# Third group of token tiles multiplied as one unit of 384 columns, the products of ones between the tiles removed, 72 put ahead of the first, and a new order of the whole program

## What is computed

```python
u = rmsnorm(x, norm_g)
proj = u @ w_in                       # 1024 -> 8704 columns
lx, lg, sb, scg, sh, sg, q, qg, mg = jnp.split(proj, SPLIT_POINTS, axis=-1)
# A: causal conv(4) -> gated linear recurrence, SiLU gate
xc = causal_dwconv(lx, lru_buf, lru_conv_w) + lru_conv_b
hs = rglru(xc, lru_h, ...);  z_a = (hs * silu(lg)) @ lru_wo
# B: B * conv3(C * h), SiLU gate
z_b = (silu(sg) * sb * causal_dwconv(scg * sh, sc_buf, sconv_w)) @ sconv_wo
# C: cross-attention of 4 heads into 256 memory tokens, SiLU gate
z_c = (softmax(q @ mem_k.T / sqrt(128)) @ mem_v * silu(qg)) @ xa_wo
y = (g_a * z_a + g_b * z_b + g_c * z_c) @ w_out;  out = rmsnorm(x + y, final_norm_g)
```

## Time and profile before

| what | value |
|---|---|
| median of 3 runs | 723.51 us (722.99 to 723.92) |
| the profiled execution, its own time | 723.84 us |
| its span on the slowest core, 5 | 722.2 us (the cores: 719.7 to 722.2) |
| TensorE busy | 700.2 us, 97% of the span |
| VectorE, ScalarE, GpSimd busy | 402.2, 336.9, 172.8 us |
| chain of work that ended last | 93% TensorE |

### The profile page before, as it was taken

How to read it: one execution, slowest core, us unless ns; L and a number is a source line. 1 busy time by engine, 2 the same in 40 slices (tenths; PEclk the granted TensorE clock), 3 DMA queues, 4 the chain that set the end, 5 groups by cost and what they waited for, 6 DMA issues and landing times.

```text
span 722.2 us, 13551 instructions; the slowest of 8 cores (719.7 to 722.2 us)
## 1 busy us (share of the span) xinstructions
PE 700.2 (97%) x5097; PEld 462.7 (64%) x5097; DVE 402.2 (56%) x416; ACT 336.9 (47%) x435; POOL 172.8 (24%) x210
## 2 busy tenths in 40 slices
PE   4899999999999999999999999999999999999996
PEld 3887766666666666666666666666666666665443
DVE  3545206566958869886866879732213312134667
ACT  2664426888986795885931121231221121210535
POOL 3432200000000000000000635644516270732000
PEclk9999999999999999999999999999999999999998
DMA  8972493133133322343043677662356392277736
GB/s 190 259 217 31 106 157 90 30 63 56 17 54 59 58 40 52 57 70 49 10 107 55 121 177 178 143 100 37 46 77 105 49 136 45 30 170 235 239 140 241
DMA packets 32416, 73.99 MB, mean 102 GB/s; under 512 B 4464, under 2 KB 8880, under 8 KB 32096
## 3 DMA queue, kind: packets, MB, share of 16 engines
q0 software_dynamic: 18000, 31.60, 30.3%
q1 hardware_dynamic: 14352, 41.52, 17.7%
HBM read 90.73 MB, written 9.88 MB: 139 GB/s over the span
## 4 chain that ended last, share of the span: by engine, by line
PE 93%; DMA 3%; ACT 1%; DVE 1%; issue 1%; SPq 0%; POOL 0%; ACTq 0%; DVEq 0%; POOLq 0%
PE PP L739 75%; PE PP L1348 8%; PE PP L783 6%; PE PP L834 1%; DMA R<-xp 1%; DMA R<-memp 1%; PE PP L1092 1%; PE PP L1026 1%; PE PP L1113 1%; DMA R<-w_in 1%; DVE R L842 1%; ACT R L822 0%; PE PP L1227 0%; PE PP L1100 0%; ACT R L1078 0%
## 5 line engine op out<-in xcount | busy, mean ns | idle before, releaser
L739 PE MATMUL PP<-R 128*128 128x344 bf16 x3768 | 557.3, 309 | 1.6 <-ACT R L947 0.5
L739 PEld LDWEIGHTS PP<-R 128*128 128x128 bf16 x3768 | 366.9, 98 | 187.5 <-issue 6.9
L1285 ACT ACTIVATE R<-PP 128x688 f32<-128x688 f32 x72 | 53.4, 745 | 219.9 <-PE PP L739 197.4
L1294 DVE SCALAR_TENSOR_TENSOR R<-R,PP 128x688 f32<-128x688 f32 x72 | 62.5, 869 | 133.8 <-PE PP L739 130.1
L141 POOL DMA_DIRECT2D R<-w_in x68 | 39.1, 575 | 294.8 <-PE PP L739 196.4
L783 PE MATMUL PP<-R 128*128 128x128 bf16 (+3 forms) x672 | 56.6, 242 | 4.0 <-issue 2.0
L1348 PE MATMUL PP<-R 128*128 128x512 bf16 x256 | 55.4, 379 | 0.0
L783 PEld LDWEIGHTS PP<-R 128*128 128x128 bf16 x672 | 46.6, 100 | 11.1 <-issue 5.2
L1298 POOL TENSOR_TENSOR R<-R 128x688 f32<-128x688 f32 x24 | 40.5, 1687 | 20.8 <-DVE R L1294 20.4
L1303 POOL TENSOR_TENSOR R<-R 128x688 bf16<-128x688 f32 x24 | 42.3, 1772 | 12.8 <-DVE R L1294 11.2
L1348 PEld LDWEIGHTS PP<-R 128*128 128x128 bf16 x256 | 25.0, 98 | 30.1
(11 more groups left out here) (139 smaller groups left out, 517.7 us busy)
## 6 DMA issues: line engine op xcount, KB each, us to landing
R<-w_in POOLq DMA_DIRECT2D x68, 256.0 KB, 4.5
R<-xp SPq DMA_DIRECT2D x32, 512.0 KB, 9.1
R<-ck SPq DMA_DIRECT2D x16, 512.0 KB, 4.8
y_p<-R SPq DMA_DIRECT2D x16, 512.0 KB, 3.3
R<-R SPq DMA_DIRECT2D x64, 64.0 KB, 2.0
R<-cv POOLq DMA_DIRECT2D x16, 256.0 KB, 7.5
R<-w_out POOLq DMA_DIRECT2D x8, 256.0 KB, 7.4
R<-xa_wo POOLq DMA_DIRECT2D x14, 128.0 KB, 3.0
```

The source lines that it names most:

```text
L739: return lambda e: e.matmul(ps.ap[:, b * 512:b * 512 + BLK], lhs(k), rhs[:, k, c:c + BLK], start=(k == 0), stop=(k == nk - 1))
L1285: G.act(lambda e, ps=pg[u], th_=th_: e.activation(out=b3(th_.ap), in_=pv(ps), func=AF.Tanh, scale=0.5), UW, [pg[u].tok], [th_.tok], Px - E ...
L1294: G.dve(lambda e, zp=zp, th_=th_, dst=dst: e.scalar_tensor_tensor(out=b3(dst.ap), in0=b3(th_.ap), scalar=1.0, in1=pv(zp), op0=ALU.add, op1 ...
```

## The change

- `BYTILE` is 2: the third group (tiles 6, 7 and 8, columns 768 to 1152) of the seven finely cut projections is 8 products of 384 columns instead of 24 of 128.
- `FILL` is empty: no product of ones between or behind the tiles.
- `WARM` = 72 products of ones run ahead of the transposes of tile 0.
- The planner gets a table of arrivals (`ARRIVE`), by which in its model the first loads of a queue land no sooner, another cost for VectorE's product L1185 (1190 instead of 1024), and a new table `SHIFT`. These emit nothing; they set the order.

```diff
-WARM = 96
-FILL = (5, 5, 3, 2)
+WARM = 72
+ARRIVE = {
+    "sp": (5.0, 5.2, 9.5, 13.8, 16.8, 20.2, 23.1, 26.6, 29.8, 33.2, 36.2, 39.3, 42.4, 45.8, 48.8),
+    "pool": (9.1, 13.1, 16.4, 19.5, 22.8, 26.2, 29.4, 33.4, 36.9, 40.1, 43.4, 47.0),
+}
+FILL = ()
-BYTILE = 3
+BYTILE = 2
 SHIFT = {
-    "x0.act": 8, "x0.pool": -123, "x0.dve": 89.5, "x0.pe": -77, "x1.act": 138.5, "x1.pool": 52.5, "x1.dve": -97, "x1.pe": -87.5,
+    "first0.pool": -16.5, "x0.act": -1, "x0.pool": -16, "x0.dve": -1, "x1.act": -30, "x1.pool": -52, "x1.dve": 44.5, "x1.pe": -35.5,
...
+        landed = {q: list(v) for q, v in ARRIVE.items()}
...
+                if start < 58.0 and landed[q]:
+                    fin = max(fin, landed[q].pop(0))
...
-        G.pe([lambda e: e.matmul(warm.ap[:, 0:128], onesb, onesb, start=True, stop=True) for _ in range(1)], 7.0, [m_ones.t], [warm.tok], -300)
+        G.pe([lambda e: e.matmul(warm.ap[:, 0:128], onesb, onesb, start=True, stop=True) for _ in range(WARM)], 0.1, [m_ones.t], [warm.tok], -300)
...
-                    in1=qs.unsqueeze(1).to_broadcast([128, 8, 128]), op=ALU.mult), 1024, [k_.tok, m_qs.t], [pr_.tok], P1)
+                    in1=qs.unsqueeze(1).to_broadcast([128, 8, 128]), op=ALU.mult), 1190, [k_.tok, m_qs.t], [pr_.tok], P1)
```

More of the change, by code:

```diff
@@ L221 @@
 SHIFT = {
[12 rows of a table removed]
-    "kv.pool": 8.5, "kv.pe": 13, "kv.act": -10.5, "kv.sp": 29, "kv.dve": 89.5, "gates0.pe": 14, "gates0.act": 48, "rec0.act": -20.5,
[59 rows of a table removed]
[9 rows of a table added]
+    "x18.dve": 6, "x18.pe": 18.5, "states.sp": -13, "states.dve": -1, "states.act": 52, "states.pool": 19.5, "heads_q0.act": -4.5,
+    "heads_q1.pe": 16.5, "heads_q1.act": -2, "heads_q2.pe": 25.5, "heads_q2.act": -83.5, "heads_q3.pe": 22.5, "qs.dve": -1, "qs.pe": 50.5,
+    "A_lg0.pe": 58, "A_lg0.act": 158.5, "B_sg0.pe": -3, "A_lx0.dve": -8, "A_lx0.pe": -35.5, "A_lx0.act": -100, "conv0.act": -70.5,
+    "conv0.dve": -135.5, "kv.pool": 27, "kv.pe": 0.5, "kv.act": 2.5, "kv.sp": 9, "kv.dve": 2, "gates0.pe": -2.5, "gates0.act": -10.5,
[58 rows of a table added]
 }
@@ L838, in p0 @@
                 fill = Handle(PS, 1)
-                t = G.pe([lambda e, fill=fill: e.matmul(fill.ap[:, 0:128], onesb, onesb, start=True, stop=True) for _ in range(1)], 0.224,
+                t = G.pe([lambda e, fill=fill: e.matmul(fill.ap[:, 0:128], onesb, onesb, start=True, stop=True) for _ in range(4)], 0.224,
                          [m_ones.t], [fill.tok], 900)
```

## The result

The changed kernel takes 724.73 us, the median of 20 runs, beside 723.63 us for the kernel before, also 20 runs: the ratio is 1.0016, with a 95% interval of 1.0009 to 1.0024. So it is slower by about 1.2 us, less than the 0.2% that I had called no change, but on the other side of zero from the forecast of 1.0 us gained. (Two of the 20 executions, of 765 and 766 us, were disturbed on one half of the chip and are in no ratio.)

The account below looks back on a forecast made before the run. TensorE was taken as the bound, busy 700.2 of 722.2 us. Gains of 0.27 + 0.17 + 0.6 = 1.0 us off the median of 723.51 gave 722.5 us, range 720.0 to 725.5.

Parts of the forecast that it names:

- The rest of the order: Whole program: waits redrawn by the new order (`SHIFT`), taken as 0; bounds 1.5 us gained, 4 lost.
- First and second term: Where TensorE is full: fewer products through 384 columns, 0.27 us gained; three late products of ones dropped, 0.17 us.
- The front: Start up to tile 7: dropping the ones between tiles changes nothing; bounds 0.5 us gained, 1.0 lost.
- The instruction blocks: TensorE's early gaps awaiting instructions: 1.4 us against 2.03, 0.6 gained; bounds 2.0 gained, 1.0 lost.
- Rival 1: Faster: instruction gaps go on all cores, and some small waits too; 720.6 or 720 us, chance 0.32.
- Rival 2: At merge00: last recurrence comes late, a stall of 3 us gives 725.5; chance 0.16, including other waits this size.
- Rival 3: At the front: TensorE's clock falls again without ones between tiles, 1.6 us late at tile 7; 724.7 us, chance 0.12.

Follow-up runs that it names:

- before_again: The kernel before, run again with no edit; 723.45 us, ratio 0.9997.
- held_one: held_early with one product of ones at the start instead of 72; 721.71 us, ratio to the kernel before 0.9970.
- held_early: Changed kernel with six xp loads held until the fourth fix product is done and merge10's w_in load issued one GpSimd sum earlier; 721.56 us, ratio 0.9971.
- held_ones: held_early with 68 products of ones put back between the first tiles, where TensorE was idle; 722.09 us, ratio to the kernel before 0.9982.
- w_early: Changed kernel with only merge10's w_in load issued ahead of one GpSimd sum, 4.3 us earlier; 725.22 us, ratio to the kernel before 1.0014.

## Why the prediction was wrong

**The time**: 722.5 forecast, 724.73 measured, inside the range of 720.0 to 725.5, and near the price of the slower rivals.

**The step that failed** is "The rest of the order: I take 0". It has two parts, and both are real. The small waits of the old order are gone, which is what its lower bound promised: 0.17, 0.17, 0.41 and 0.49 us of core 3 are down to nothing. But the new order brought waits for loads, 2.0 to 4.2 us in sum on one core of each pair, and the time is that of the slowest core. I had put the bounds at 1.5 gained and 4 lost, which held, and had bounded the loss by a VectorE scan. I looked for the late result on VectorE and ScalarE and didn't look at how much earlier than its first product each weight load is issued on GpSimd, nor at what SyncE issues beside it. Both can be read from the new order: three GpSimd sums directly ahead of merge10's load and six ck loads around it, six xp loads directly beside the fix loads. What no row of the old kernel shows is how much longer a load takes in such company; the runs show 6.3 to 6.7 us instead of 2.7 to 3.0 for 128 KB on the later cores.

**The choice of 0 from what the old order showed** was the error in reasoning. That an order by the same planner had 1.6 us of waits says nothing about the next one: the planner models one core, and has no term for what its neighbour loads.

**First and second term**: 384 columns cost 162.5 ns in the changed kernel too (16 products from 41.32 to 43.92 us on core 3), no ones lie in the full stretch. Right, as far as the trace can show.

**The front**: forecast 0 with 1.0 lost as the bound; 0.76 us later on core 3. Of the idle time reckoned from tile 1 on, core 3 has 0.62 and 0.92 us behind the transposes of tiles 1 and 2, where I took 1.0 each; the 0.8 and 1.1 us ahead of tiles 2 and 3 didn't come, since TensorE with its slow products was itself the later one.

**The instruction blocks**: the forecast named the place, 123 products behind the first, behind tile 6's transposes, and none at 24 us. Right on both. The size was 0.71 us where I took 1.4 against 2.03 before. By the longest gaps of the two profiled executions the term gained 1.3 instead of 0.6, but the 2.03 was one execution's: before_again has 1.21 at most. Nor are these gaps the whole difference between the old kernel's cores, as I had it: core 5 is 2.5 us longer than core 3 and its gap 2.03, core 1 is 0.4 longer with a gap of 0.63. That the ones at the start are what removes the first gap I can't maintain: held_one has 1 product of ones and no gap there, so the new order does it, or chance.

**Rival 1** happened on the short cores: 718.5 to 719.2 us, below the best core before. It is what the kernel would be without the load waits, as held_early shows.

**Rival 2**, the last recurrence late to merge00, didn't happen: no wait there on any core. The time to spare was enough; how much of the 3.3 us was left isn't measured. The price of 725.5 was nearly right by luck, for another mechanism made the kernel slower.

**Rival 3**, the clock falls again, happened, and cost half of what I gave it, 0.76 instead of 1.6 us at tile 7: on core 3 some six eights went at the slow pitch, and not sixteen, for the products are fast again from about 19 us on. The Trainium skill (TensorE: Matmul & The Clock Gate, Part 1) has TensorE fall back to half rate when it is idle; here the rows at 13.46 and 15.95 agree. With held_ones, where the clock stays up, the spans don't fall, so this rival was right in its mechanism and not what made the kernel slower.

**Core 3 by these terms**: -0.27 - 0.17 + 0.76 - 1.24 + 0.11 (the last wait of the tail, 2.96 instead of 2.85) = -0.8 us; measured 719.7 to 719.2, -0.5. The 0.3 us between them aren't explained.

## What to carry to other kernels

When an order is made anew, list for every load the time from its issue to its first use and what else is issued beside it on any queue, and compare the shortest ones with the old order: a 128 KB load with 4.7 us of lead was in time alone on every core, and 1.6 to 2.0 us late on four of eight beside six loads of 512 KB. Bulk loads for a later stage are best tied to the end of the last small load's use, not left to whenever their buffers come free. Look at all cores of a profile, not at the slowest: a difference between neighbours that the program doesn't make points to something they share.

## What was unexpected of the hardware

- Of two neighbouring cores one was later in all 72 pairs of the changed kernel, by 3.0 us in the median, where both run the same program on their own data. It is not always the same one. With the two colliding loads untangled the difference is 0.5 us. That they share a path to memory is the reading that fits; no run measured that path itself. The Trainium skill (HBM Reference, Specifications) says that the two cores of a pair share the bandwidth of their memory, and advises to measure a change in transfers with both cores active. That the spans differ by pairs agrees with it; what either core of a pair got of the memory wasn't measured.
- A wait of TensorE in the middle of the kernel can cost more than itself. Behind 2.00, 2.34 and 2.80 us of idleness 32 products of 344 columns took 6.47 to 6.50 instead of 4.83 us (w_early), at a granted clock of 0.67 and 0.77 in the windows behind the last of these, and behind 5.60 us the clock was at 0.50. The length of the wait alone doesn't decide it: behind 1.96, 2.25 and 2.32 us the products were slow too, and behind 2.11, 2.29 and 2.30 us they were not.
- The gaps for instructions, wherever one of at least 0.2 us was seen in twelve profiles of two orders and their variants, stand at nearly fixed counts of products, about 125 apart; where they fall in time is a matter of what is put ahead.
